# A mixture-of-experts stage on one Trainium2 core: 47 blocks of 32 slots in place of 39 blocks of 64, and overflow blocks whose weights are loaded on a condition

## The reference, cut to what matters

```python
MOE_GROUPS, MOE_PER_GROUP, MOE_EXPERTS, MOE_TOPK, MOE_HIDDEN = 4, 8, 32, 2, 256

def _moe(x, wr_g, br_g, wr_e, br_e, w_gate, w_up, w_down):
    def one_seq(xs):                                   # xs: 256 x 1024
        pg = softmax(xs @ wr_g + br_g)                 # 4 groups
        ptop, gsel = top_k(pg, 1)
        le = (xs @ wr_e + br_e) of the chosen group    # 8 experts
        lv, esel = top_k(le, MOE_TOPK)
        we = softmax(lv) * ptop
        gate = we at the two chosen experts, 0 elsewhere   # 256 x 32
        hg = einsum('sd,edh->seh', xs, w_gate)
        hu = einsum('sd,edh->seh', xs, w_up)
        h = silu(hg) * hu * gate[..., None]
        return einsum('seh,ehd->sd', h, w_down)
```

## Time and profile before

| | |
|---|---|
| time, median of 3 runs (lowest, highest) | 2059.68 us (2059.26, 2061.4) |
| the profiled execution: its own time | 2055.11 us |
| its span | 2053.3 us |
| mean granted clock of TensorE, as a share of full speed | 0.946 |
| HBM read over the span | 322.56 MB |
| expert stage: first product to the last scatter | 533.4 us to 891 us of the span |

### The profile page before, as it was taken

One profiled execution on the slowest core, in us unless ns is written; L12 is line 12 of the kernel. 1 busy time (PEld: TensorE's weight loads), 2 busy tenths in 40 slices (PEclk: granted clock), 3 DMA queues, 4 the chain that ended last, 5 costly groups with the idle time before them and its releaser, 6 DMA issues.

```text
span 2053.3 us, 32139 instructions
## 1 busy us (share of the span) xinstructions
PE 1836.2 (89%) x12472; PEld 1407.5 (69%) x12472; DVE 955.0 (47%) x1706; ACT 730.7 (36%) x1346; POOL 117.2 (6%) x162
## 2 busy tenths in 40 slices
PE   7987685997899999969999989999998889979997
PEld 7934445996454444548777858878876775779997
DVE  3452635665412211133644455534543455458684
ACT  4433213443111111133266353333333534555454
POOL 0100000004000000020000110000001100010000
PEclk9998896998899999989999989999999899989998
DMA  6886482554599999842200212222222230135552
GB/s 244 194 325 218 169 304 76 184 183 124 196 357 340 354 353 347 326 157 83 82 11 1 72 62 93 93 92 93 92 92 83 82 103 0 42 113 173 184 181 68
DMA packets 91036, 325.88 MB, mean 159 GB/s; under 512 B 10832, under 2 KB 12880, under 8 KB 90768
## 3 DMA queue, kind: packets, MB, share of 16 engines
q1 hardware_dynamic: 86832, 313.04, 43.9%
q0 software_dynamic: 2736, 7.35, 1.6%
q10 hardware_dynamic: 1328, 3.53, 0.4%
HBM read 322.56 MB, written 3.15 MB: 159 GB/s over the span
## 4 chain that ended last, share of the span: by engine, by line
PE 74%; DMA 12%; DVE 8%; ACT 4%; issue 2%; POOL 0%; SPq 0%; DVEq 0%; ACTq 0%; POOLq 0%
PE bank L739 47%; PE bank L684 15%; DMA ring<-wall 12%; PE bank L1186 4%; PE bank L1157 3%; PE bank L763 2%; PE bank L1170 2%; DVE w_lo L1783 1%; ACT BIG L1442 1%; DVE BIG L2340 1%; PE bank L1208 1%; ACT w_hi L1382 0%; PE bank L1214 0%; ACT L1444 0%; ACT XC L1450 0%
## 5 line engine op out<-in xcount | busy, mean ns | idle before, releaser
L739 PE MATMUL bank<-BIG_f32r,w_hi 128*128 128x256 f32 (+1 forms) x2208 | 551.9, 339 | 27.1 <-DVE BIG_f32r L1796 17.1
L1783 DVE TENSOR_TENSOR w_lo<-ring,w_hi 128x1024 fp32r<-128x1024 f32 x261 | 325.1, 1256 | 297.6 <-ACT w_hi L1382 295.7
L739 PEld LDWEIGHTS bank<-BIG_f32r,w_hi 128*128 128x128 f32 x2208 | 382.4, 192 | 77.1 <-issue 28.3
L739 PE MATMUL bank<-BIG_f32r,w_lo 128*128 128x256 f32 (+1 forms) x1136 | 385.9, 340 | 0.0
L1382 ACT ACTIVATE w_hi<-ring 128x1024 fp32r<-128x1024 f32 x261 | 272.6, 1054 | 223.6 <-PE bank L739 213.6
L739 PE MATMUL bank<-AR_f32r,w_hi 128*128 128x256 f32 (+1 forms) x1066 | 270.2, 332 | 16.8 <-issue 9.4
L739 PEld LDWEIGHTS bank<-BIG_f32r,w_lo 128*128 128x128 f32 x1136 | 218.2, 192 | 25.0 <-issue 0.2
L739 PEld LDWEIGHTS bank<-AR_f32r,w_hi 128*128 128x128 f32 x1066 | 186.1, 193 | 37.4 <-issue 9.9
L1157 PE MATMUL bank<-ring,AR 128*64 128x256 f32 x1248 | 158.0, 386 | 27.6 <-DMA ring<-wall 26.1
L1157 PEld LDWEIGHTS bank<-ring,AR 128*64 128x64 f32 x1248 | 82.6, 136 | 114.2 <-DMA ring<-wall 59.0
L739 PE MATMUL bank<-AR_f32r,w_lo 128*128 128x256 f32 (+1 forms) x448 | 148.3, 331 | 0.0
(11 more groups left out here) (355 smaller groups left out, 2334.2 us busy)
## 6 DMA issues: line engine op xcount, KB each, us to landing
ring<-wall SPq DMA_DIRECT2D x595, 512.0 KB, 5.0
BIG<-t_rows POOLq DMA_DIRECT2D x16, 128.0 KB, 13.5
AR<-na_rows POOLq DMA_DIRECT2D x32, 64.0 KB, 2.5
con<-consts ACTq DMA_DIRECT2D x1, 1794.0 KB, 12.0
na_rows<-rpb_pad POOLq DMA_DIRECT2D x1, 1792.0 KB, 33.8
XC<-xin ACTq DMA_DIRECT2D x1, 1024.0 KB, 6.3
XC<-ctxin POOLq DMA_DIRECT2D x1, 1024.0 KB, 5.9
out<-XC SPq DMA_DIRECT2D x8, 128.0 KB, 1.8
```

What stands on the lines that cost most here:

```text
L739: ins = nc.tensor.matmul(o, l, r, start=start and n == 0, stop=stop and n == 2, **kw)
L1783: V.tensor_tensor(w_lo[:, i % SPLIT_RING, :], ring[:, t % RING, :], w_hi[:, i % SPLIT_RING, :].bitcast(F32), ALU.subtract).then_inc(w_spli ...
```

## The change

SLOTS becomes 32, so that there can be EXTRA = 512 // 33 = 15 overflow blocks and there are 47 blocks. `moe_blocks` puts an overflow block after every second expert (0, 1, X0, 2, 3, X1, ..., 28, 29, X14, 30, 31). `moe_up` uses four column groups: 8 products of 512 columns, each group adding two of the eight slices of the contraction; `moe_fold` (4 products with a constant, 32 columns moving) adds the four groups and transposes in one step. `moe_down` uses four column groups of 256 columns, `moe_scatter` four row groups of 32 rows.

The ring carries the tiles of experts 1 to 31 alone. Six tile buffers `w_extra` lie over `w_hi` and `w_lo`, which nothing else uses in this stage. Expert 0's tiles are loaded there when the stage before has used its last split tile. Before each overflow block SP waits until the previous user of `w_extra` is done, reads two registers, and issues six loads on a condition: with `needed` = 0 they move nothing and only count up the semaphore. ACT's first split of `l0in` now waits for the last `moe_down`.

```diff
-SLOTS = 64
+SLOTS = 32
...
-    order += [("moe", 6 * MOE_BLOCKS)]
+    order += [("moe", 6 * (EXPERTS - 1))]
...
+def moe_blocks():
+    order = []
+    for e in range(EXPERTS):
+        order.append(e)
+        if e % 2 and e // 2 < EXTRA:
+            order.append(EXPERTS + e // 2)
+    return order
...
 def moe_stream():
+    order, items = moe_blocks(), []
+    for i, b in enumerate(order + [None]):
+        if b is not None and 0 < b < EXPERTS:
+            items += [(b, q) for q in range(4)]
+        if i and 0 < order[i - 1] < EXPERTS:
+            items += [(order[i - 1], 4), (order[i - 1], 5)]
+    return items
...
+        w_extra = nc.alloc_sbuf_tensor_at("w_extra", [P, 6, TILE], F32, offset=nc.sbuf_base - 4 * 2 * SPLIT_RING * TILE)
...
+            extra_from = {(max(moe_order[i - 2], 1), 5): i for i, b in enumerate(moe_order) if b >= EXPERTS}
+
+            def load_extra(i):
+                n = moe_order[i] - EXPERTS
+                if n == 0:
+                    sp.wait_ge(w_used, last_split_use)
+                    for q in range(6):
+                        sp.dma_start(w_extra[:, q, :], wall[moe0 + q]).then_inc(extra_ready[q], 16)
+                    sp.wait_ge(sem("moe_table"), 1)
+                sp.wait_ge(sem("moe_y"), moe_order.index(EXPERTS + n - 1 if n else 0) + 1)
+                expert = sp.value_load(i_experts[0:1, n:n + 1], min_val=0, max_val=EXPERTS - 1)
+                needed = sp.value_load(i_needed[0:1, n:n + 1], min_val=0, max_val=1)
+                for q in range(6):
+                    sp.dma_start(w_extra[:, q, :], wall[expert * 6 + (moe0 + q)], cond=needed,
+                                 bounds_check="skip_entire_dma").then_inc(extra_ready[q], 16)
...
                     sp.dma_start(ring[:, t % RING, :], src).then_inc(w_ready[t % RING], 16)
+                    if in_moe and (b, q) in extra_from:
+                        load_extra(extra_from[b, q])
...
+            def moe_weights(n, q):
+                b = moe_order[n]
+                if 0 < b < EXPERTS:
+                    return tile("moe", tile_at[b, q])
+                release()
+                pe.wait_ge(extra_ready[q], 16 * (b - EXPERTS + 2 if b else 1))
+                return w_extra[:, q, :]
+
             def moe_up(n):
...
+                    g, c0 = k % 4, (k % 2) * 512
+                    ins = nc.tensor.matmul(ps[0][32 * g:32 * g + 32, :], Xb[:, n % 2, k, :], w[:, c0:c0 + 512],
+                                           start=k < 4, stop=k >= 4, tile_position=(0, 32 * g))
...
+            def moe_fold(n):
+                pe.wait_ge(sem("moe_h"), n + 1)
+                if n:
+                    pe.wait_ge(sem("moe_hid"), n)
+                for c in range(4):
+                    ins = nc.tensor.matmul(ps[1][:, c * SLOTS:(c + 1) * SLOTS], m_h[:, c * P:(c + 1) * P], c_("fold"),
+                                           start=True, stop=True)
+                ins.then_inc(sem("moe_tr"), 1)
...
             def moe_down(n):
...
+                    for g in range(4):
+                        ins = nc.tensor.matmul(ps[2][32 * g:32 * g + 32, 0:S], m_hT[:, n % 2, k, :],
+                                               w[:, g * S:(g + 1) * S], start=k == 0, stop=k == 1,
+                                               tile_position=(0, 32 * g))
...
+                for c in range(2):
+                    for g in range(4):
+                        r = slice(32 * g, 32 * g + 32)
+                        ins = nc.tensor.matmul(ps[4 + g][:, c * S:(c + 1) * S], m_y[r, c * P:(c + 1) * P],
+                                               m_selT[r, n % 3, :], start=False, stop=n == MOE_BLOCKS - 1 and c == 1,
+                                               skip_group_check=True, tile_position=(32 * g, 0))
...
-                f(m_h, ps[0][:, 0:S], ACT.Copy).then_inc(sem("moe_h"), 1)
+                f(m_h, ps[0], ACT.Copy).then_inc(sem("moe_h"), 1)
...
+            act.wait_ge(sem("moe_y"), MOE_BLOCKS)
             feed("l0in", 0)
...
+            step(V.tensor_scalar(r_few[:, 7, :], whose, float(EXPERTS), None, ALU.is_lt))
+            step(V.tensor_copy(i_needed, r_few[:, 7, :]))
...
-                    V.tensor_copy(m_y, ps[2]).then_inc(sem("moe_y_out"), 1)
+                    V.tensor_copy(m_y, ps[2][:, 0:S]).then_inc(sem("moe_y_out"), 1)
```

More of the change, by code:

```diff
@@ L310, in build @@
         i_experts = aM.take(EXTRA).bitcast(I32)
+        i_needed = aM.take(EXTRA).bitcast(I32)
         sel = aM.take_f32r(2, 512)
@@ L313, in build @@
         Xb = aM.take(2, KC, SLOTS)
-        m_h = aM.take(S)
+        m_h = aM.take(512)
         m_sg = aM.take(2, SLOTS)
         m_hT = aM.take(2, 2, SLOTS)
-        m_y = aM.take(512)
-        m_sel = aM.take(2, 2, 2 * SLOTS)
+        m_y = aM.take(S)
+        m_sel = aM.take(2, 2, 4 * SLOTS)
         m_selT = aM.take(3, S)
@@ L376, in build @@
         w_ready = [sem(f"weights_in_slot{s}") for s in range(RING)]
+        extra_ready = [sem(f"extra_weights_in_slot{q}") for q in range(6)]
+        moe_order = moe_blocks()
+        last_split_use = split_at[first["out"] + stage_tiles["out"] - 1] + 1
         w_free = sem("ring_slots_freed")
@@ L567, in _ @@
                 in_moe = moe0 <= t < moe1
-                back = pad if t >= moe1 else 0
+                ahead = 6 if t >= moe1 else 0
                 rounds = 0 if in_moe else (end - t) // RING
@@ L573, in _ @@
                             sp.wait_ge(freed, r * RING + (place[old] + q + 1))
-                            sp.dma_start(ring[:, (t + q) % RING, :], wall[r * RING + (t - back + q)])\
+                            sp.dma_start(ring[:, (t + q) % RING, :], wall[r * RING + (t + ahead + q)])\
                                 .then_inc(w_ready[(t + q) % RING], 16)
@@ L577, in _ @@
                 while t < end:
-                    src = wall[t - back]
+                    src = wall[t + ahead]
                     if in_moe:
                         b, q = stream[t - moe0]
[L581 to L588, removed]
+                        src = wall[moe0 + 6 * b + q]
                     sp.wait_ge(freed, place[t - RING] + 1)
                     sp.dma_start(ring[:, t % RING, :], src).then_inc(w_ready[t % RING], 16)
+                    if in_moe and (b, q) in extra_from:
+                        load_extra(extra_from[b, q])
                     t += 1
@@ L1153, in moe_up @@
                 for k in range(KC):
[L1154 to L1162, removed]
+                    if k % 2 == 0:
+                        w = moe_weights(n, k // 2)
+                    g, c0 = k % 4, (k % 2) * 512
+                    ins = nc.tensor.matmul(ps[0][32 * g:32 * g + 32, :], Xb[:, n % 2, k, :], w[:, c0:c0 + 512],
+                                           start=k < 4, stop=k >= 4, tile_position=(0, 32 * g))
+                    if k == KC - 1:
+                        ins.then_inc(sem("moe_gu"), 1)
+                    else:
+                        note(ins, None)
+            def moe_fold(n):
[6 more added lines that the diff above has]
+                ins.then_inc(sem("moe_tr"), 1)
             def moe_down(n):
@@ L1181, in moe_scatter @@
                 pe.wait_ge(sem("moe_y_out"), n + 1)
[L1182 to L1190 removed]
+                for c in range(2):
[4 more added lines that the diff above has]
+                                               skip_group_check=True, tile_position=(32 * g, 0))
+                        if c and g == 3:
                             ins.then_inc(sem("moe_out"), 1)
@@ L2541, in shape_constants @@
     put("pick", pick.reshape(P, 4))
+    put("fold", np.tile(np.eye(32), (4, 1)))
     return c
```

60 lines of the change are left out of this document (18 added, 42 removed).

## The result

The changed kernel takes 2003.66 us (median of 4 runs, 2000.84 to 2008.29) against 2059.47 us for the kernel before on the same chip (4 runs, 2058.86 to 2061.4): ratio 0.973, 95% interval 0.9713 to 0.9747. It is faster by 55.8 us, where 71.5 were forecast. The profiled execution took 2002.8 us with a span of 2001.0.

A forecast was written before the change was run, and what follows sets the result against it. The expert stage was taken as bound by its tile loads, PE close behind. Moving its end from 890.99 to 818.4 saves 72.6 us from 2055.1, giving 1982.5; 4.6 to the median and 1 for SP make 1988 us, range 1964 to 2018.

The forecast's parts named there:

- Tiles, removed: Expert stage's ring loads: 228 become 180, expert 0's six hidden ahead; 48 fewer at 1.494 us save 71.7 us.
- PE's work: PE per expert-stage block: up 1.85, scatter 1.0, down 0.93, selection 0.31, fold 0.93, together 5.0 us; 15.0 a cycle.
- The rival by which PE becomes the bound: Expert stage: blocks cost 6.5 us, 2014 us in all; decides from 6.0 us a block; chance 0.14.
- SP's queue: Conditional loads hold SP 3.0 us a cycle between ring loads; counted as 0, upper bound 1 us a cycle, 15 in all.
- The loads' rate: Expert stage's ring: 1.494 us a tile at 351 GB/s, 17.9 us for the 12 tiles of two experts.
- Ahead of the stage: DVE's longer tables before the experts add 2.9 us, taken up by 3.0 us of DVE's waits for PE.
- The start: Up(0) stays at 533.42 us; first of 180 tiles issued at 545.5, after down(0), and landing at 548.8.
- The end: Last tile lands at 816.2 us; half a down, copy, handovers and scatter bring the residual's start to 818.4, from 890.99.
- more than 301 MB read: Sign in the changed profile that the forecast was wrong; HBM reads were expected at 300.5 MB.
- Fuller queue: Expert stage's load rate rises to 388 GB/s, 1.351 us a tile; 1961 us; chance 0.10.
- A skipped load holds SP for 1 us: Conditional loads in SP's queue: the cycle grows to some 21 us, 46 us back, about 2034 us; chance 0.07.
- The other side, loads not skipped: Overflow blocks' 90 tiles all move: 2122 us, 62 slower than before; slower from eight of fifteen blocks on; chance 0.05.

The follow-up runs named there:

- reads_before_wait: Against the changed kernel, SP reads both registers before it waits for the overflow block's down, not after; 2002.98 us, ratio 0.9733.
- the two by ACT: Against the changed kernel, ACT instead of SP issues the conditional loads: six of 512 KB, 1996.99 us; twelve of 256 KB, 2009.81 us.
- all_loads_taken: Against the changed kernel, the condition is always true, so all 15 overflow blocks load their six tiles; 2105.32 us in one run.
- act_six_loads: Against the changed kernel, ACT instead of SP issues the six conditional loads of 512 KB; 1996.99 us, ratio 0.9681.
- one_conditional_load: Against the changed kernel, SP issues one conditional load of 3 MB in place of six of 512 KB; 1997.33 us, ratio 0.9704.
- act_and_early_release: Against the changed kernel, ACT issues one 3 MB conditional load and the last tiles of up and down are released sooner; 1994.9 us, ratio 0.9706.
- conditional_load_by_act: Against the changed kernel, ACT reads the registers, waits for down and issues one 3 MB conditional load; SP only streams; 1996.21 us, ratio 0.9714.

## Why the prediction was right, and where its sum was off

- **Tiles, removed: right.** 180 loads carry the stage, six more move bytes ahead of it, 90 move none. The packets show it.
- **PE's work: right.** Up 1.83 (forecast 1.85), scatter 1.07 (1.0), fold 0.92 (0.93), selection 0.35 (0.31), down 0.91 (0.93): 5.08 us a block where 5.0 was forecast. The scatter's price was right, its reading of the loads was not:

```profile
698.73 0.74 PEld L1231 LDWEIGHTS bank<-AR 32*128 32x128 f32 x16 [0.84 <-issue]
...
L1231 PEld LDWEIGHTS bank<-AR x60: 181/184/185, 693.6 to 711.9; 32*128 32x128 f32 x60
...
699.80 0.97 PEld L1206 LDWEIGHTS bank<-con,AR 128*128 128x128 f32 x8 [0.33 <-ACT AR L1676]
```

  One load of 32 x 128 takes 184 ns (the middle of 181/184/185), and so did each of the 14 of the earlier trace rows, not 54. Full loads of 128 x 128 have a median of 192 ns. What differs is the overlap: sixteen loads spread over four row groups take 0.74 us together, eight full ones 0.97. The Trainium skill ("TensorE: Matmul & The Clock Gate", LDWEIGHTS) says that the rows don't change a load's time, and 184 against 192 agrees; its figure of about 107 ns is near what eight full loads in a row give (0.97 / 8 = 0.12 us), and not a price for loads of different row groups in a row (0.74 / 16 = 0.05 us). The rival by which PE becomes the bound fell with it.
- **SP's queue: the hold was nearly right, its counting at 0 was not.** SP was held 3.45 us (3.0 forecast): 1.46 us passed before the first issue where 0.4 was put for the reads, of which the reads are 0.1 by reads_before_wait, and the six issues were 0.33 us apart, not 0.44. The six conditional loads together cost 0.4 us a cycle: three kernels with them in SP's queue have 18.96 to 19.02 us and 2002.98 to 2003.84, two without any have 18.57 and 18.66 us, and 1994.37 and 1996.85. Whether it is SP's hold or the loads themselves is open, since every run that took one away took most of the other with it, or was blurred (the two by ACT).
- **The loads' rate: the term that was mis-sized.** 17.9 us for the tiles of a cycle was taken from the windows of before and held for the new order too. The cycle measured 19.02: 15 x 1.1 = 16.5 us. The runs split it in three: 0.1 us by which the tiles of two blocks took longer than forecast even without any of the new (17.93 against 18.06), 0.6 from the interleaving (18.06 against 18.66) and 0.4 from the six conditional loads (18.66 against 19.02), 2, 9 and 5 us over the stage. The prediction had priced SP's lateness alone, at 0 with 1 us a cycle as the upper bound, because PE's slack of 2.9 us a cycle seemed to leave room. The interleaving, the larger part, it hadn't named at all. That slack helps little: the tiles are asked for when slots come free, and during an overflow block none does. That the bound of 15 us came close to the 16.5 is thus in part luck. 2003.66 lies just outside the likeliest case's span of 1981 to 2003 and inside the range. The prediction's own terms, 5 us for the rate and 15 for SP upon 1988, would have carried that span to 2008.
- **Ahead of the stage: right.** DVE's four copies ran back to back (2.48 us, no wait where there were 3.0 us of them), so the tables' longer operations (0.66 us each for 480 elements) were hidden, to within the 0.5 us or so by which the drift in the next point grows up to the stage.
- **The start: 0.6 us off, beside a drift of 3.2.** Up(0) came 3.2 us later, but an ACT operation on a bank far ahead of it, in untouched code, was already at 349.60 where it had been at 346.94, 2.7 us of the 3.2; over the experiments' profiles up(0) lies anywhere from 528.9 to 542.6. The first of the 180 tiles was issued at 549.36, forecast 545.5, of which 0.6 isn't that drift. The first overflow block also waited 2.00 us for its skipped loads, a wait that the prediction did not have.
- **The end.** 838.99 instead of 818.4 is 20.6 us: 3.2 + 0.6 + 16.5 = 20.3. The time forecast from the span was 72.6 us off; 52.3 came.
- **The sign "more than 301 MB read" was a wrong test.** The counter showed 347.74 MB though nothing more was read. Only the packets tell.
- **The rivals.** Fuller queue: it fell in this kernel (334 GB/s), but the 367 GB/s of all_loads_taken shows that more in flight does fill it, and by that run the 358 that the Trainium skill ("DMA: Bandwidth & Descriptors", specifications) names as a core's limit, half of what two cores share, is no ceiling here, where one core runs alone. A skipped load holds SP for 1 us: it fell, 0.33 us. The other side, loads not skipped, was forecast at 2122 and measured at 2105 when forced; it was 17 us cheaper, as the rate rose to 367. The prediction's turning point has a slip: 72.6 us are 48.6 tiles at its own price, so nine overflow blocks and not eight would make the kernel slower. The clock stayed at 1.00, 2.4 GHz, in the window.

Open: whether the six conditional loads cost by SP's hold of 3.45 us or by themselves, and by what mechanism. An experiment that holds SP for 3.45 us without issuing a load would tell. The interleaving's 0.6 us rests on one run of the order with the experts first, and that it costs because an overflow block frees no slot is argued: it fits the estimates of loads on the way, but no run shows it by itself. Among the versions that keep the overflow path, act_six_loads (0.9681), one_conditional_load (0.9704), act_and_early_release (0.9706) and conditional_load_by_act (0.9714) lie below the changed kernel's 0.973; their intervals overlap it, but their stages, 291 to 298 us against 302, agree in sign. One conditional load is the least edit and keeps ACT free.

## What to carry to other kernels

When a stream of loads is the bound, take its rate from a stretch with the same number of tiles in flight and the same pattern of release: here 17.9 us of tiles became 19.0, more than half of it because blocks that load nothing came between. Six loads under a condition are not free when skipped, 0.4 us a cycle here, and one large one costs about half of that or less, so issue one. Put the work that needs no load between blocks that do, since 0.6 us of lost rate bought 5 us of PE's time. And look in the trace of an experiment whether the edit moved what it was to move, and what else it moved. Here the reads put ahead of the wait moved SP's first issue by 0.1 us and not by 1.4, and twelve loads by ACT made ACT's copy late, so neither run settles what it was built for.

## What the runs showed of the hardware that was not expected

- A skipped load is counted as read: the HBM counter was 47.2 MB too high (90 x 524288 bytes), and showed the same 347.74 MB when all 90 did move. The packets were right, 303.95 and 351.14 MB.
- Six skipped loads a cycle, issued by the engine that issues the ring's, cost 0.4 us of a cycle of 19 (18.96 to 19.02 us with them, 18.57 and 18.66 without). One of 3 MB cost 0.2 us or less (18.82, 18.61, 18.69).
- The rate of the same 512 KB loads was 334 GB/s (share 0.90) with a ring of six interrupted by blocks that free nothing, 347 (0.94) uninterrupted, and 367 (0.98) with up to twelve on the way, over 340 us.
- From the end of a down to SP's first conditional issue 1.46 us passed, and 1.37 with both register reads ahead of the wait; a conditional issue with an address from a register took 0.33 us, whether for 512 KB by SP or 256 KB by ACT. One of 3 MB took 0.09.
- A weight load of 32 x 128 took 184 ns, one of 128 x 128 a median of 192; sixteen of the former, in four row groups, took 0.74 us together, eight of the latter 0.97.
